# Layer 1's neighbourhood attention on tiles of 8 rows by 16 columns, with the bias table laid out on the host

## The chip, the cores and the metric

One core of a Trainium2 chip runs the whole program in one launch. The time is that of the device in microseconds, from the launch to the end, median of three runs. All inputs start in HBM. Arrays may be laid out anew on the host before the launch; that is not timed, and no arithmetic on input values is done there. Matrix products run in a 32-bit form in which each operand is split into a rounded high part and a rest, so that one product is three: high x high, high x low, low x high.

## The reference

Two blocks of two layers each. The change is in the second layer of the first block: 512 latent tokens on a grid of 8 rows by 64 columns, 256 context tokens, 8 heads of 128 features. With eight rows the row window of 8 is the whole grid, so a query at column c sees all rows, 16 neighbouring columns, and the whole context:

```python
def neighbourhood_attention(q, k, v, k_ctx, v_ctx, rpb):
    ...
    cols = np.arange(GRID_W)                                  # 64
    c_start = np.clip(cols - WIN_C // 2, 0, GRID_W - WIN_C)   # 16 columns from here
    col_mask = (cols[None, :] >= c_start[:, None]) & (cols[None, :] < c_start[:, None] + WIN_C)
    dc_idx = np.clip(cols[None, :] - cols[:, None] + WIN_C - 1, 0, 2 * WIN_C - 2)
    rpb_c = rpb[:, :, dc_idx]
    def row_block(r):
        ...
        s_lat = jnp.einsum('bhqd,bhrkd->bhqrk', q_r, k_b).astype(f32) * scale + bias.astype(f32)
        s_lat = jnp.where(col_mask[:, None, :], s_lat, -jnp.inf).reshape(b, h, GRID_W, wr * GRID_W)
        s_ctx = jnp.einsum('bhqd,bhkd->bhqk', q_r, k_ctx).astype(f32) * scale
        p = jax.nn.softmax(jnp.concatenate([s_lat, s_ctx], axis=-1), axis=-1).astype(v.dtype)
        ...
```

Queries and keys are projections of the normed tokens, normed again per head; the output goes through an output projection.

## The kernel before

Each of the five engines runs a fixed program in the order in which it is written; they wait for each other on semaphores. Weights stream through two slots: SP loads 512 KB into `raw`, ACT rounds it to `w_hi` (L330), POOL computes the rest `w_lo` (L390).

`pe_near`, `act_near` and `dve_near` are the attention of this layer. They walk over 8 heads `e` with five projection items `i` each, and over 32 units `u`, four a head, one for each block of 128 queries. A unit of head e - 1 is worked on behind an item of head e. TensorE does, in this order:

- `item(e, i)`: the projection, 8 x 3 products over the features. i = 0 is the queries (512 columns), 1 and 2 the keys, 3 and 4 the values; the 768 tokens are cut in two thirds of 384 columns (`third_at`, `THIRD`).
- `post(at)`: for queries and keys the sum of the squares over the features (a product with ones, L2424), for values three transposes (L2428).
- `step(u)`, in four of the five rounds: `turn(u - 1)` transposes the probabilities of the last unit (6 blocks, L2437), `scores(u)` makes the scores of the next (L2449, 3 products over 256 context keys and 3 over 512 latent keys), `weigh(u - 1)` multiplies the transposed probabilities with the values (6 products, L2460). `near_order` gives the unit; behind item 3 there is none.

DVE copies items out of PSUM (`evict`, L2576), finishes norms (`finish`: reciprocal L2588 and multiply L2589), makes low parts (`low`, L2594), and for a unit negates and takes the minimum of the scores with the bias table added (`shift`, L2603 and L2604), scales by the inverse sum (`normalise`, L2612), and copies the result out (`take`, L2617). ACT squares (L2511), takes roots (L2520), rounds (L2525), copies the transposes out of PSUM (`copy`, L2531), takes the exponential (L2536), and rounds the next weights in rounds 0, 2 and 4.

The queries of a unit are two grid rows. The bias table `bt` holds for each of the 64 key columns and 120 pairs of head and row distance a value per query; it is made at the start of the stage from the 120 x 31 parameters by 256 small products with a band of ones (`bias` in `pe_near`, L2381), and DVE adds the column mask as it copies it (`bias` in `dve_near`, L2568). These calls stand between the items of head 0. After the last item the units 28 to 31 have no items beside them: `step` is followed by products of the output projection (`out_part`, L2371), and `hold` (L397) puts in products of the identity with itself. Then the output projection goes on at L425.

## Time and profile before

| | us |
|---|---|
| median of three runs | 3625.74 (3624.43 to 3628.43) |
| span of the profiled execution | 3613.9 |
| PE busy | 3486.9 (96%) |
| DVE busy | 1619.4 (45%) |
| ACT busy | 1223.8 (34%) |
| POOL busy | 1173.4 (32%) |

The span is that of one profiled execution, from its first to its last instruction; the profile gives no other time for it, and the launch and the end of the program lie around it. Matmul times overlap, since the next begins while the last one drains: what one costs is read from the start of one to the start of the next. The chain that ended last is 51% issue, 21% PE, 19% POOL and 6% DVE.

### The profile page before, as it was taken

The page shows a single profiled execution, that of the slowest core. Times are in us where ns is not written, and L with a number is a line of the kernel's source. Part 1 is how long each engine was busy: PE and PEld are TensorE (multiplying, and loading weights), DVE is VectorE, ACT ScalarE, POOL GpSimd, SP SyncE. Part 2 cuts the span into 40 slices and gives each one's busy share as a digit, 9 for nine tenths or more (in the row PEclk, how much of TensorE's full clock was granted, in tenths as well). Part 3 has the DMA queues.
Part 4 walks back from the last instruction along what each step waited for, and adds up shares of the span by engine and source line. Part 5 has one row for each costly group of instructions (what it writes and reads, how often), then busy time and mean ns, then how long its engine had stood idle before and what let it go on. Part 6 is the DMA issues. An engine that isn't in the chain of part 4 may idle for free.

```text
span 3613.9 us, 61844 instructions
## 1 busy us (share of the span) xinstructions
PE 3486.9 (96%) x24970; PEld 3053.1 (84%) x24970; DVE 1619.4 (45%) x2762; ACT 1223.8 (34%) x1848; POOL 1173.4 (32%) x812
## 2 busy tenths in 40 slices
PE   8999988889999999999999999999999999999998
PEld 6777878878888888889888888978999999778887
DVE  6966644446220222666662135455512355564121
ACT  4545432233111111455532223255312232542222
POOL 1221122223222233111155454213444432145453
PEclk9999999999999999999999999999999999999999
DMA  5320000001432421111133232112222321123332
GB/s 229 112 70 25 32 2 2 2 25 59 174 110 91 154 86 60 41 42 42 45 96 101 88 104 75 59 48 65 88 93 87 99 70 53 48 76 94 98 93 93
DMA packets 65341, 273.80 MB, mean 76 GB/s; under 512 B 9856, under 2 KB 11008, under 8 KB 62080
## 3 DMA queue, kind: packets, MB, share of 16 engines
q1 hardware_dynamic: 61280, 268.58, 22.4%
q8 instruction: 144, 2.36, 0.3%
q10 hardware_dynamic: 3872, 2.49, 0.2%
q14 instruction: 45, 0.37, 0.0%
HBM read 268.95 MB, written 2.10 MB: 75 GB/s over the span
## 4 chain that ended last, share of the span: by engine, by line
issue 51%; PE 21%; POOL 19%; DVE 6%; ACT 1%; POOLq 0%; PEld 0%; PEldq 0%; DVEq 0%; ACTq 0%
POOL w_lo L390 18%; PE ps L407 10%; PE ps L1488 3%; DVE arena L1776 1%; DVE arena L1762 1%; PE ps L506 1%; PE ps L1998 1%; PE ps L1571 0%; PE ps L2004 0%; DVE arena L1832 0%; PE ps L1549 0%; PE ps L1903 0%; POOLq L385 0%; POOL delta_bufs L2295 0%; DVE arena L1781 0%
## 5 line engine op out<-in xcount | busy, mean ns | idle before, releaser
L390 POOL TENSOR_TENSOR w_lo<-raw,w_hi 128x512 fp32r<-128x512 f32 (+1 forms) x760 | 1101.0, 1469 | 2169.9 <-ACT w_hi L330 2169.9
L330 ACT CAST w_hi<-raw 128x1024 fp32r<-128x1024 f32 (+1 forms) x380 | 419.6, 1104 | 1583.1 <-PE ps L407 1262.7
L407 PE MATMUL ps<-act_hi,w_hi 128*128 128x512 f32 (+2 forms) x2048 | 579.0, 337 | 9.3 <-POOL w_lo L390 3.7
L407 PE MATMUL ps<-act_lo,w_hi 128*128 128x512 f32 (+2 forms) x2048 | 576.8, 336 | 0.0
L407 PE MATMUL ps<-act_hi,w_lo 128*128 128x512 f32 (+2 forms) x2048 | 576.5, 336 | 0.0
L407 PEld LDWEIGHTS ps<-act_hi,w_hi 128*128 128x128 f32 x2048 | 360.1, 188 | 63.3 <-issue 23.5
L407 PEld LDWEIGHTS ps<-act_hi,w_lo 128*128 128x128 f32 x2048 | 362.4, 188 | 41.9
L407 PEld LDWEIGHTS ps<-act_lo,w_hi 128*128 128x128 f32 x2048 | 362.2, 188 | 40.9
L407 PE MATMUL ps<-ff_hi,w_hi 128*128 128x512 f32 (+2 forms) x1056 | 297.1, 336 | 0.0
L407 PE MATMUL ps<-ff_hi,w_lo 128*128 128x512 f32 (+2 forms) x1056 | 297.0, 336 | 0.0
L407 PE MATMUL ps<-ff_lo,w_hi 128*128 128x512 f32 (+2 forms) x1056 | 297.0, 336 | 0.0
L2753 PE MATMUL ps<-act_hi,w_hi 128*128 128x272 f32 (+1 forms) x896 | 265.2, 296 | 0.0
L2753 PE MATMUL ps<-act_lo,w_hi 128*128 128x272 f32 (+1 forms) x896 | 253.8, 283 | 0.0
L2753 PE MATMUL ps<-act_hi,w_lo 128*128 128x272 f32 (+1 forms) x896 | 253.7, 283 | 0.0
L780 DVE TENSOR_TENSOR nscr<-nscr,ps 128x256 f32<-128x256 f32 (+2 forms) x66 | 34.8, 556 | 436.0 <-PE ps L407 436.0
L407 PEld LDWEIGHTS ps<-ff_lo,w_hi 128*128 128x128 f32 x1056 | 186.5, 188 | 21.1
L407 PEld LDWEIGHTS ps<-ff_hi,w_hi 128*128 128x128 f32 x1056 | 186.5, 188 | 20.9
L407 PEld LDWEIGHTS ps<-ff_hi,w_lo 128*128 128x128 f32 x1056 | 186.5, 188 | 20.8
L2753 PEld LDWEIGHTS ps<-act_hi,w_hi 128*128 128x128 f32 x896 | 169.3, 189 | 10.3 <-issue 5.9
L2753 PEld LDWEIGHTS ps<-act_lo,w_hi 128*128 128x128 f32 x896 | 169.4, 189 | 0.9
L2753 PEld LDWEIGHTS ps<-act_hi,w_lo 128*128 128x128 f32 x896 | 169.5, 189 | 0.0
L725 DVE TENSOR_TENSOR nscr<-nscr,ps 128x512 f32<-128x512 f32 (+2 forms) x50 | 26.4, 556 | 315.8 <-PE ps L407 287.5
(495 smaller groups left out, 6249.1 us busy)
## 6 DMA issues: line engine op xcount, KB each, us to landing
raw<-in_gu SPq DMA_DIRECT2D x176, 512.0 KB, 3.5
arena<-in_ada SPq DMA_DIRECT2D x24, 2048.0 KB, 7.8
raw<-in_dn SPq DMA_DIRECT2D x64, 704.0 KB, 4.1
raw<-in_in SPq DMA_DIRECT2D x56, 512.0 KB, 3.5
raw<-in_even_in SPq DMA_DIRECT2D x28, 512.0 KB, 3.5
raw<-in_odd_in SPq DMA_DIRECT2D x24, 512.0 KB, 3.5
raw<-in_out SPq DMA_DIRECT2D x16, 512.0 KB, 3.6
raw<-in_even_out SPq DMA_DIRECT2D x8, 512.0 KB, 3.5
```

The costliest lines, as they stand in the source:

```text
L330: act.copy(w_hi[:, j, 0:cols], raw[:, j, 0:cols]).then_inc(s["hi_ready"], 1)
L390: ins = pool.tensor_tensor(w_lo[:, j, c], raw[:, j, c], w_hi[:, j, c].bitcast(F32), ALU.subtract)
L407: mm = pe.matmul(ps[:, 2 * j + b, 0:cn], wt[:, j, w], acts[:, k, c0:c0 + cn], start=(k == 0 and wt is w_hi and acts is hi), stop=(k == kt ...
L506: mm = pe.matmul(ps[:, 2 * j + b, 0:cn], wt[:, j, w], acts[:, k, c0:c0 + cn], start=(k == 0 and wt is w_hi and acts is hi), stop=(k == KD ...
L725: ins = dve.tensor_tensor(nscr[:, 1, h0:h0 + hn], nscr[:, 0, h0:h0 + hn], ps[:, 2 + b, 0:hn], ALU.mult)
L780: ins = dve.tensor_tensor(nscr[:, 1, h0:h0 + hn], nscr[:, 0, h0:h0 + hn], ps[:, 2 + b, 0:hn], ALU.mult)
L1488: mm = pe.matmul(ps[:, h, 0:cn], wt[:, b % 2, w], a[:, k, c0:c0 + cn], start=(k == 0 and wt is w_hi and a is act_hi), stop=(k == KD - 1 an ...
L1762: ins = dve.scalar_tensor_tensor(acc, gd[:, m, j:j + GN], v("conv", 5 * m + j), acc, ALU.mult, ALU.add)
L1776: dve_link(dve, n, dve.reciprocal(r, r))
L1998: mm = pe.matmul(pblk(2, d, e, b), blk(DEC_B if l % 2 else LAB_B, d, e, b), blk(X, d, e, b), start=True, stop=True)
L2753: mm = pe.matmul(ps[:, h, 0:cn], wt[:, b % 2, w], a[:, k, TOK2 + c0:TOK2 + c0 + cn], start=(k == 0 and wt is w_hi and a is act_hi), stop=( ...
```

## The change

A unit is now a tile of 8 grid rows by 16 grid columns. Its 128 queries have all eight rows, and the key columns in reach are 24 (first and last block) or 32 (the two in the middle), which is 192 or 256 latent keys where there were 512. To make these keys contiguous, tokens are stored by octets of columns: `evict` writes an item of 512 columns in the order octet, row, column in the octet. The values are stored with the last octet first, so that the copy of item 4 is two instructions; `PIECES` says for each block which value tiles and rows its four blocks of probabilities meet. `take` writes the results back in the order of the grid.

The items are cut at the border of context and latent: 512 queries, 512 latent keys, 256 context keys, 256 context values, 512 latent values. The round without a step is that of the context keys (i = 2). Scores of a unit lie in one PSUM bank, its transposes too, and units take turns between two banks. `turn` and `weigh` have 4 products, the exponential and the scaling 448 or 512 columns.

The bias is the same for all blocks up to the mask, because a query sees the same relative columns. The host lays the parameters out as 128 x 2048 values (copies and zeros only); ACT's queue loads them where it loaded the parameters, and DVE adds the masks for three kinds of block in ten instructions (`tables`). The bias products, their semaphores and the band of ones are gone.

```diff
+    cmask = []
+    for block, first, octets in ((1, -1, 4), (0, 0, 3), (3, -1, 3)):
+        q = 16 * block + 8 * (i // 64) + i % 8
+        start = np.clip(q - 8, 0, 48)[:, None]
+        kk = 16 * block + 8 * first + np.arange(8 * octets)[None, :]
+        cmask.append(np.where((kk >= start) & (kk < start + 16), 0.0, -BIG))
...
-        bt = arena[:, 0:120 * 64].rearrange("p (s c) -> p s c", c=64)
+        near_bias = arena[:, 0:2048]
+        near_tables = [(near_bias.rearrange("p (e o t) -> p e o t", e=8, o=4), cmask[0]),
+                       (arena[:, 2048:3584].rearrange("p (e o t) -> p e o t", e=8, o=3), cmask[1]),
+                       (arena[:, 3584:5120].rearrange("p (e o t) -> p e o t", e=8, o=3), cmask[2])]
...
+        NEAR_COLS = (None, (CTX, LAT), (0, CTX), (0, CTX), (CTX, LAT))
...
+            return rows.rearrange("p (o r j) -> p r o j", o=8, r=8)
...
+        KEYS = ((0, 192), (64, 256), (192, 256), (320, 192))
+        PIECES = (((0, 0, None), (P, 1, None), (CTX - 64, 5, 64), (CTX + 64, 2, None)),
+                  ((0, 0, None), (P, 1, None), (CTX, 2, None), (CTX + P, 3, None)),
+                  ((0, 0, None), (P, 1, None), (CTX, 3, None), (CTX + P, 4, None)),
+                  ((0, 0, None), (P, 1, None), (CTX, 4, None), (CTX + P, 5, 0)))
 
         def near_unit(u):
 
-            e, t = u // 4, u % 4
-            j0 = 15 * e + 7 - 2 * t
-            return e, t * P, bt[:, j0:j0 + 8, :].rearrange("p s c -> p (s c)")
+            e, b = u // 4, u % 4
+            k0, kn = KEYS[b]
+            table = near_tables[{0: 1, 3: 2}.get(b, 0)][0]
+            return e, b, CTX + k0, kn, table[:, e].rearrange("p o t -> p (o t)")
 
         def near_order(e, i):
 
-            u = 4 * (e - 1) + (i if i < 3 else i - 1)
-            return None if i == 3 or e == 0 else u
+            u = 4 * (e - 1) + (i if i < 2 else i - 1)
+            return None if i == 2 or e == 0 else u
...
-            def bias(g):
...
             def turn(u, beats=0):
-                if u >= 1:
-                    pe.wait_ge(s["near_copied"], u)
-                hold(pe, beats, 4)
+                if u >= 2:
+                    pe.wait_ge(s["near_copied"], u - 1)
+                hold(pe, beats, 4 + u % 2)
                 pe.wait_ge(s["near_p"], u + 1)
-                for t in range(6):
-                    mm = pe.transpose(ps[:, 4 + t // 4, (t % 4) * P:(t % 4 + 1) * P], near_z[:, u % 2, t * P:(t + 1) * P], ident)
+                for t, (c, _, _) in enumerate(PIECES[u % 4]):
+                    mm = pe.transpose(ps[:, 4 + u % 2, t * P:(t + 1) * P], near_z[:, u % 2, c:c + P], ident)
                 mm.then_inc(s["near_turned"], 1)
...
-                if u >= 1:
-                    pe.wait_ge(s["near_top"], u)
-                else:
-                    pe.wait_ge(s["bt_read"], 16)
-                for b, (k0, kn) in enumerate(BOTH):
+                if u >= 2:
+                    pe.wait_ge(s["near_top"], u - 1)
+                for z0, c0, cn in ((0, 0, CTX), (CTX, k0, kn)):
                     for q, k in ((q_hi, k_hi), (q_lo, k_hi), (q_hi, k_lo)):
-                        mm = pe.matmul(ps[:, 2 + b, 0:kn], q[:, e % 2, q0:q0 + P], k[:, e % 2, k0:k0 + kn],
+                        mm = pe.matmul(ps[:, 2 + u % 2, z0:z0 + cn], q[:, e % 2, b * P:(b + 1) * P], k[:, e % 2, c0:c0 + cn],
...
-                for t in range(6):
-                    mm = pe.matmul(ps[:, 6, 0:P], near_v[:, e % 2, t, :], near_pt[:, u % 2, t * P:(t + 1) * P],
-                                   start=(t == 0), stop=(t == 5))
+                for t, (_, tile, half) in enumerate(PIECES[u % 4]):
+                    rows = slice(0, P) if half is None else slice(half, half + 64)
+                    mm = pe.matmul(ps[:, 6, 0:P], near_v[rows, e % 2, tile, :], near_pt[rows, u % 2, t * P:(t + 1) * P],
+                                   start=(t == 0), stop=(t == 3))
...
-                act.copy(near_pt[:, u % 2, 0:T], ps[:, 4:6, :].rearrange("p a t -> p (a t)")[:, 0:T]).then_inc(s["near_copied"], 1)
+                act.copy(near_pt[:, u % 2, 0:4 * P], ps[:, 4 + u % 2, :]).then_inc(s["near_copied"], 1)
...
+                z = near_z[:, u % 2, 0:CTX + KEYS[u % 4][1]]
...
-            def bias(g):
-                dve.wait_ge(s["bt_ready"], g + 1)
-                c = slice(4 * g, 4 * g + 4)
-                dve.tensor_tensor(bt[:, :, c], ps[:, 2 + g % 4, 0:480].rearrange("p (c s) -> p s c", c=4),
-                                  cmask[:, c].unsqueeze(1).to_broadcast([P, 120, 4]), ALU.add).then_inc(s["bt_read"], 1)
+            def tables(i):
+                whole = near_tables[0][0]
+                if i == 1:
+                    dve.wait_ge(s["rpb_landed"], 16)
+                kind = i % 3
+                table, mask = near_tables[kind]
+                for o in range(table.shape[2]):
+                    cube = lambda a: a.rearrange("p e (r j) -> p e r j", j=8)
+                    ins = dve.tensor_tensor(cube(table[:, :, o]), cube(whole[:, :, o + (1 if kind == 1 else 0)]),
+                                            mask[:, 8 * o:8 * o + 8].unsqueeze(1).unsqueeze(1).to_broadcast([P, 8, 8, 8]), ALU.add)
+                if i == 3:
+                    dve_link(dve, n, ins)
 
             def evict(at):
                 _, cn, dst = near_item(at // ITEMS, at % ITEMS)
                 dve.wait_ge(s["item_done"], at + 1)
                 if at >= ITEMS and at % ITEMS >= 3:
                     dve.wait_ge(s["post_done"], at - ITEMS + 1)
-                dve.tensor_copy(dst, ps[:, item_bank(at), 0:cn]).then_inc(s["item_read"], 1)
+                src = ps[:, item_bank(at), 0:cn]
+                if cn == LAT:
+                    dst, src = by_octets(dst), by_rows(src)
+                if at % ITEMS == 4:
+                    dve.tensor_copy(dst[:, :, 1:8], src[:, :, 0:7])
+                    dst, src = dst[:, :, 0], src[:, :, 7]
+                dve.tensor_copy(dst, src).then_inc(s["item_read"], 1)
...
+                z, bank = near_z[:, u % 2, :], ps[:, 2 + u % 2, :]
+                dve_link(dve, n, dve.tensor_scalar(z[:, 0:CTX], bank[:, 0:CTX], -1.0, None, ALU.mult, ALU.min, accum_out=small[:, 4:5]))
+                dve.tensor_tensor_reduce(z[:, CTX:CTX + kn], bank[:, CTX:CTX + kn], table, -1.0, small[:, 4:5], ALU.add, ALU.min,
                                          small[:, u % 2:u % 2 + 1]).then_inc(s["near_top"], 1)
...
-                dve.tensor_copy(near_mix[:, e, q0:q0 + P], ps[:, 6, 0:P]).then_inc(s["near_taken"], 1)
+                rows = near_mix[:, e].rearrange("p (r b o j) -> p b r o j", r=8, b=4, o=2)[:, b]
+                dve.tensor_copy(rows, ps[:, 6, 0:P].rearrange("p (o r j) -> p r o j", o=2, r=8)).then_inc(s["near_taken"], 1)
 
             for e in range(8):
                 for i in range(ITEMS):
                     at = ITEMS * e + i
                     u = near_order(e, i)
                     evict(at)
-                    if e == 0:
-                        for g in range(4 * i, min(4 * i + 4, 16)):
-                            bias(g)
+                    if e == 0 and 1 <= i <= 3:
+                        tables(i)
...
-                act.dma_start(pa[0:31, 1:121], dram["rpbT"]).then_inc(s["rpb_landed"], 16)
+                act.dma_start(near_bias, dram["rpb"]).then_inc(s["rpb_landed"], 16)
...
+    def near_table(z):
+
+        wide = np.zeros((8, 15, 47), np.float32)
+        wide[:, :, 8:39] = z
+        rows = [wide[:, 7 - r:15 - r, 15 - 8 * o - j:47 - 8 * o - j] for o in range(2) for r in range(8) for j in range(8)]
+        return np.stack(rows).reshape(P, 8, 8, 4, 8).transpose(0, 1, 3, 2, 4).reshape(P, 2048)
```

On ACT, head 1, from the exponential behind item 2 to that behind item 4, before (`arena<-ps,eps_t` is a root, `arena,small<-arena,small` an exponential, ACT_TABLE_LOAD the change of function table between the two):

```order
L2536 ACT_TABLE_LOAD
L2536 ACTIVATE arena,small<-arena,small 128x768 [waits near_top]
L2520 ACT_TABLE_LOAD [waits normed]
L2520 ACTIVATE arena<-ps,eps_t 128x384 [waits post_done]
L2525 CAST near_parts<-arena 128x384 [waits normed]
L2531 COPY arena<-ps 128x768 [waits near_out,near_turned]
L2525 CAST near_parts<-arena 128x384 [waits normed]
L330 CAST w_hi<-raw 128x1024 [waits w_landed1,item_done]
L2536 ACT_TABLE_LOAD
L2536 ACTIVATE arena,small<-arena,small 128x768 [waits near_top]
```

And now, from the root of the context keys behind item 3 to the exponential behind item 4:

```order
L2505 ACTIVATE arena<-ps,eps_t 128x256 [waits normed,post_done]
L2516 COPY arena<-ps 128x512 [waits near_turned]
L2510 CAST near_parts<-arena 128x512 [waits normed]
L2521 ACT_TABLE_LOAD
L2521 ACTIVATE arena,small<-arena,small 128x512 [waits near_top]
L2516 COPY arena<-ps 128x512 [waits near_out,near_turned]
L2510 CAST near_parts<-arena 128x256 [waits normed]
L326 CAST w_hi<-raw 128x1024 [waits w_landed1,item_done]
L2521 ACTIVATE arena,small<-arena,small 128x448 [waits near_top]
```

The last root now stands in a round that has a step, ahead of its exponential, and the exponential of the round of item 4 follows without a change of table.

On TensorE, the work between the third and the fourth item of head 0 before (L2424 the sum of squares, L2381 the bias products):

```order
L2381 MATMUL ps<-pa,base 64x120 [waits scaled_ready]
L2381 MATMUL ps<-pa,base 64x120 x15
L2424 MATMUL ps<-arena,base 128x512 [waits square_ready]
L2381 MATMUL ps<-pa,base 64x120 [waits bt_read]
L2381 MATMUL ps<-pa,base 64x120 x7
```

And now this place and the next two follow-ups, with the items between them left out:

```order
L2417 MATMUL ps<-arena,base 128x512 [waits square_ready]
...
L2417 MATMUL ps<-arena,base 128x512 [waits square_ready,post_read]
L2417 MATMUL ps<-arena,base 128x256 [waits square_ready,post_read]
...
L2422 MATMUL ps<-base,arena 128x128 [waits item_read,post_read]
L2422 MATMUL ps<-base,arena 128x128
```

Nothing stands any more between an item's sum of squares and the next item.

## Rows read from the trace of the kernel before

**Rows 1.** Busy time by stretches: stretch, length, engines (instructions), clock, DMA share, GB/s

```profile
core 0: us, PE busy (x) PEld busy (x) DVE busy (x) ACT busy (x) POOL busy (x), PEclk, DMA share, GB/s
1512.00:1767.00 255.00, 253.94 (x1533) 229.53 (x1532) 167.87 (x298) 152.50 (x204) 52.92 (x42) 1.00 0.15 44
1767.00:1799.00 32.00, 27.92 (x192) 23.45 (x191) 17.74 (x48) 16.80 (x27) 2.50 (x2) 1.00 0.08 20
1484.00:1487.70 3.70, 3.70 (x64) 3.54 (x61) 2.60 (x5) 0.74 (x2) 0.00 (x0) 1.00 0.42 140
1487.80:1491.20 3.40, 3.40 (x12) 3.40 (x12) 3.37 (x2) 0.00 (x0) 0.00 (x0) 0.52 0.00 0
```

**Rows 2.** PE's timeline, one round: start, duration, engine, line, operation, count, idle before

```profile
1560.14 0.42 PE L2390 MATMUL ps<-act_hi,w_hi 128*128 128x384 f32 x1
...
1564.40 0.81 PE L2424 MATMUL ps<-arena,base 128*128 128x384 f32 x2
1565.12 0.85 PE L2437 MATMUL ps<-base,arena 128*128 128x128 f32 x6
1565.72 1.30 PE L2449 MATMUL ps<-near_parts 128*128 128x256 f32 x6
1566.90 1.58 PE L2460 MATMUL ps<-arena 128*128 128x128 f32 x12
1568.23 0.42 PE L2390 MATMUL ps<-act_hi,w_hi 128*128 128x384 f32 x1
```

**Rows 3.** ACT's timeline, the copy of the same round

```profile
1566.00 0.80 ACT L2531 COPY arena<-ps 128x768 f32<-128x768 f32 x1 [0.17 <-PE ps L2437]
```

**Rows 4.** PE's timeline, the scores of unit 0 and of unit 27

```profile
1511.81 1.29 PE L2449 MATMUL ps<-near_parts 128*128 128x256 f32 x6
...
1767.05 1.30 PE L2449 MATMUL ps<-near_parts 128*128 128x256 f32 x6
```

**Rows 5.** PE's timeline in the feed-forward ahead, pairs of 256 and 512 columns

```profile
1450.12 0.51 PE L407 MATMUL ps<-ff_hi,w_lo 128*128 128x256 f32 x2
1450.46 0.51 PE L407 MATMUL ps<-ff_hi,w_hi 128*128 128x256 f32 x2
```

**Rows 6.** ACT's groups by form, 1445 to 1800: count, busy us, mean ns, idle before

```profile
L2520 ACT ACT_TABLE_LOAD x21 | 26.9, 1283 | 0.4
...
L2520 ACT ACTIVATE arena<-ps,eps_t 128x384 f32<-128x384 f32 x16 | 9.3, 583 | 35.2 <-PE ps L2424 35.2
...
L2520 ACT ACTIVATE arena<-ps,eps_t 128x512 f32<-128x512 f32 x8 | 5.5, 687 | 22.4 <-PE ps L2424 22.4
```

**Rows 7.** DVE's groups by form, 1445 to 1800

```profile
L2588 DVE RECIPROCAL arena<-arena 128x512 f32<-128x512 f32 x8 | 26.8, 3347 | 0.0
...
L2568 DVE TENSOR_TENSOR arena<-ps,base 128x480 f32<-128x480 f32 x16 | 10.4, 657 | 6.6 <-PE ps L2381 6.6
...
L2594 DVE TENSOR_TENSOR near_parts<-arena,near_parts 128x384 fp32r<-128x384 f32 x16 | 8.8, 552 | 0.0
...
L2594 DVE TENSOR_TENSOR near_parts<-arena,near_parts 128x512 fp32r<-128x512 f32 x8 | 5.5, 685 | 0.0
```

**Rows 8.** DVE's groups by form, whole span

```profile
L560 DVE TENSOR_TENSOR nscr<-nscr 128x512 f32<-128x512 f32 x16 | 26.2, 1637 | 0.0
```

**Rows 9.** PE's timeline, bias products at the start of the stage

```profile
1483.53 3.50 PE L2381 MATMUL ps<-pa,base 31*64 31x120 f32 x64
1486.96 0.44 PE L2390 MATMUL ps<-act_hi,w_hi 128*128 128x384 f32 x1
```

**Rows 10.** DVE's timeline, its first copy of the stage

```profile
1479.95 0.69 DVE L2576 COPY arena<-ps 128x512 f32<-128x512 f32 x1
```

**Rows 11.** POOL's timeline

```profile
1480.34 2.50 POOL L390 TENSOR_TENSOR w_lo<-raw,w_hi 128x512 fp32r<-128x512 f32 x2 [22.03 <-ACT w_hi L330]
```

**Rows 12.** PE's timeline, turns of units 27 and 31, and the output projection

```profile
1772.73 0.87 PE L2437 MATMUL ps<-base,arena 128*128 128x128 f32 x6 [0.94 <-DVE arena L2612]
...
1793.60 0.85 PE L2437 MATMUL ps<-base,arena 128*128 128x128 f32 x6 [0.47 <-DVE arena L2612]
...
1798.81 0.47 PE L425 MATMUL ps<-act_hi,w_hi 128*128 128x512 f32 x1 [0.26 <-DVE act_lo L916]
```

85 lines of the change are left out of this document (25 added, 60 removed).

## The prediction

> **What bounds the kernel now.** I read the page's first part: PE is busy nearly the whole span, the others half of it or less, so a change pays where it takes PE time or shortens a wait of PE. The busy time by stretches then shows that the attention of layer 1, from 1512 to 1767 us, has PE at 253.9 of 255 us, DVE at 168 and ACT at 153, and the clock at 1.00 [rows 1]. PE sets the pace; DVE and ACT have a third free on the mean, which says nothing yet of the short stretches. Third, PE's own timeline of one round, for the start-to-start times (busy times of overlapping matmuls are longer than what they cost) [rows 2].
>
> I call a round one projection item with what follows it: the item, its follow-up (`post`), and a step: `turn` of the last unit (6 transposes), `scores` of the next, `weigh` of the last. In the round shown [rows 2] the item takes 1560.14 to 1564.40, the follow-up to 1565.12, `turn` 0.60 us, `scores` 1.18, `weigh` 1.33: a step is 3.11 us. From the first scores to those of unit 27 it is 1511.81 to 1767.05 [rows 4]: 255.2 us, 27 steps, 37.8 a head of four.
>
> **The steady part, per step.** Price of one instruction, start to start:
> - `weigh`: 6 products in 1.33 us, 0.222 each. Two fewer: -0.44.
> - `turn`: 6 transposes in 0.60 with the entry to them, so at most 0.10 each; I take 0.095: two fewer, -0.19.
> - `scores`: an item of 384 columns is 24 products in 4.26 us with some 0.1 of entry (1560.14 to 1564.40) [rows 2], 0.1735 each, so at most 0.45 ns a column. At the full clock of 2.4 GHz, which these rows show [rows 1], one column is 0.42 ns; I take that. Three products shrink from 512 to 256 columns (-0.32) or to 192 (-0.40), half the units each: -0.36.
>
> PE's own work would fall by 0.99 a step. But `weigh` waits for ACT's copy of the transposes, and the trace has the two nearly equal: `turn` starts at 1565.12, the copy runs 1566.00 to 1566.80 [rows 3], `weigh` starts at 1566.90 [rows 2]. After the change the transposes end 0.19 earlier; the copy of 512 columns instead of 768 costs 0.80 - 256 x 0.81 ns = 0.59, the slope from 687 against 583 ns for 512 and 384 columns [rows 6]; then 0.10 to `weigh`. That is 0.85 - 0.19 + 0.04 + 0.59 + 0.10, about 1.37 us after `turn` began, where PE alone would be through at 1.2. The copy becomes the late one: turn to weigh 1.76 to 1.37, saved 0.39, and with `weigh` 0.83 to 0.84 a step. In the round after the latent keys' item ACT has a root of 512 columns (0.69) ahead of the copy, and I take 0.69 there. Of 27 steps 7 are of that kind: 20 x 0.84 + 7 x 0.69 = **21.6 us**. Bounds: 27 x 0.99 = 26.9 if the copy delays nothing; 14 if DVE is late by 1 us in each of 7 heads besides.
>
> The items: a head had one of 512 columns and four of 384, and has three of 512 and two of 256. In the feed-forward ahead a 256 and a 512 together take 0.347 us (1450.12 to 1450.46) [rows 5], which is twice the 0.1735 of 384 columns: nothing gained or lost, items of about 5.55 and 2.98 us. Root sums and transposes after them keep their columns.
>
> What becomes late in the short rounds? I lay out one head from the end of the latent keys' item (t = 0). PE: root sums, step (`weigh` ends 3.3), context keys' item to 6.3, sums to 7.2, context values' item to 10.1, sums, step to 12.9, latent values' item to 18.4. DVE: copy out, shift of the scores to 3.2, reciprocal of 512 columns (3.35) [rows 7] and multiply to 7.2, normalise 7.8, copies to 8.4, second reciprocal and multiply to 12.4, low parts and copy to 13.3, shift to 14.2, third reciprocal (256 columns) to 16.4, normalise to 17.0. The transposes that need it stand at 18.65 in PE's queue: 1.6 us to spare. The nearest miss is the square of the context keys, ready on ACT at about 9.8 with PE asking at 10.1. So DVE is behind for ten us, and nothing waits. ACT is helped: in the order of after a head has 2 loads of the exp table and 2 of the root's where it had 3 and 3, 1.28 us each [rows 6].
>
> **The start of the stage.** 256 products for the bias table go. 64 take 3.4 us (1483.53 to 1486.96, the next item) [rows 9], 0.054 each, 13.8 in all; but the first 32 stand where PE waits for the normed activations. DVE's chain comes next, from 1479.95 [rows 10]: two copies (1.2), three table adds (0.6 each: 1.8), reciprocal and multiply (4.05), copy and three adds (2.1), second reciprocal and multiply (4.05), low parts, copy, four adds (3.3), third (2.2), the rest 2.0: near_lo stands at about 1500.7. PE: the root sums wait for squares that ACT makes only after rounding the first normed item, so PE idles 3 us near 1487 to 1490, then has two items of 5.55 and two follow-ups: scores at 1502.0. The table adds read both operands in SBUF while POOL writes low parts from 1480.34 for 2.5 us [rows 11]. A DVE add of 512 columns with two SBUF operands takes 685 ns here [rows 7] and 1637 in the feed-forwards, where POOL is at work beside it [rows 8]; I add 1.0 for it. The Trainium skill (SBUF — State Buffer, "Who interferes with whom") says that a DVE instruction with two SBUF inputs contends with a GpSimd one that reads SBUF; these rows agree. The clock: in the trace it is 0.52 from 1487.8 to 1491.2, behind 64 small bias products [rows 1], at a cost of some 1.7. With those gone and idle time in their place I expect such a stretch again, half of it behind a wait: +0.8. Scores at 1503.8 instead of 1511.81: **-8.0 us** (bounds -5.5 and -10.5).
>
> The table's load, 1 MB on ACT's queue where 15 KB went, is issued some 27 us before its first reader: the same ring moved 140 GB/s beside other work [rows 1], 7.5 us. Hidden. `base` is 57 KB shorter at the kernel's start: 0 to -0.3; I take 0.
>
> **The end of the stage.** From unit 28 on there is no projection to fill PE, and the period is a loop: turn, scores, shift, exp, normalise, turn. From turn 27 at 1772.73 to turn 31 at 1793.60 [rows 12] four periods of 5.2. Each loses 0.19 (turn), 0.32 to 0.40 (scores), 0.27 to 0.33 (DVE on fewer columns, 1.04 ns each from 685 and 552 ns for 512 and 384 [rows 7]), 0.21 to 0.26 (exp, at ACT's slope) and 0.15 (normalise): 1.15 to 1.35. The `hold` products of step 29 cut one of them; I take -5.0 for four, -0.84 behind the last (turn, copy, weigh), and -1.7 ahead of turn 27, where ACT's table load of 1.28 goes. **-7.5 us** (6 to 8.5).
>
> **Sum.** -21.6 - 8.0 - 7.5 = -37.1. The profiled span is 3613.9; launch and end lie around it, as the median of the runs, 3625.74, is 11.8 above; the same 11.8 is kept. 3625.7 - 37.1 = 3588.6.
>
> **Rivals.**
> 1. The copy delays nothing (ACT's copy is shorter than its slope says): 26.9 for 21.6. 3583.3.
> 2. Permuted access costs DVE. Copies out and `take` now write and read in runs of 8 floats. The trace has a worse pattern: the bias add read PSUM at a stride of 120 floats and wrote runs of 4, at 657 ns for 480 columns [rows 7], no slower a column than a plain add. At half pace 2560 columns a head would add 2.7 us to DVE, the square would miss by 0.4 a head, start and tail lose 2: 3593.5. By the Trainium skill (SBUF — State Buffer, "Door 1: The DMA port swizzle") each access that crosses into another 16-byte line pays; the row of the bias add doesn't show it, and the measurement decides.
> 3. The table adds meet POOL each time: 10 x (1.64 - 0.69) = 9.5 at the start, the -8.0 gone: 3598.
> 4. The clock falls once a head, for PE now waits for the copy: 7 x 1.7 = 12: 3600.5. Against it: the waits are 0.1 to 0.3 us, and PE has longer ones from 1767 to 1799, at clock 1.00 [rows 1].
> 5. Slower: the permuted writes on DVE cost what its slowest operation does, 6.5 ns a column (3347/512) [rows 7]. 2560 columns add 14 us to DVE's 25 a head (168 us over 6.75 heads [rows 1]), 39 against the 37.8 of a head now: DVE bounds the stage, +8 there, +10 at the start and end: 3644. It decides from about 5.5 ns a column on; the bias add at 1.4 speaks against it.
>
> **Chances.** Forecast 60% (its own range 3584 to 3594), rival 1 14%, 2 8%, 3 6%, 4 8%, 5 4%. Range 3580 to 3599. Runs of this kernel lie within some 0.1%, so 0.2% (7 us) is what can be told from no change: faster 0.95, same 0.01, slower 0.04.
>
> **What would show it.** Start of the first scores product near 1504, 27 steps later near 1737.5, first product of the out-projection behind the last unit, 1798.81 now [rows 12], near 1762. Steps of 2.2 to 2.3 us with `weigh` 1.35 to 1.4 after `turn`; if it is 1.2, rival 1. Permuted copies of 512 columns near 0.7 us on DVE, else 2 or 5. Table adds near 0.7, else 3. The granted clock in 40 slices shows 4. I am wrong if PE waits for DVE in the short rounds by more than 1 us a head.

## The result, and the profile after

The changed kernel takes 3591.39 us (median of four runs, 3589.48 to 3598.37) against 3625.09 of the kernel before beside it: ratio 0.9915, 95% interval 0.9901 to 0.9929, 33.7 us less. The forecast was 3588.6, 2.8 below the median.

The profiled spans, 3613.9 and 3590.6, differ by 23.3 only, so they can't be subtracted. The first copy of the stage starts at 1479.95 before [rows 10] and 1487.15 after, 7.2 us later, though nothing ahead of it was changed but a shorter constant; behind the stage another 3.4 us go the same way. The clock is 0.99 for 1.00 from 10 to 1440 us by the view of stretches: the profiled execution of before had less time at the lower level there. All that follows is measured inside the stage, from four marks that both kernels have: DVE's first copy, PE's first product of `scores(0)` and of `scores(27)`, and the first product of the output projection. In the trace of after, the first row is from DVE's timeline, the other three from PE's:

```profile
1487.15 1.29 DVE L2574 COPY arena<-ps 128x512 f32<-128x512 f32 x2
```

```profile
1510.72 0.91 PE L2441 MATMUL ps<-near_parts 128*128 128x256 f32 x6
...
1746.82 0.92 PE L2441 MATMUL ps<-near_parts 128*128 128x256 f32 x6
...
1772.10 0.47 PE L421 MATMUL ps<-act_hi,w_hi 128*128 128x512 f32 x1
```

Against rows 4, 10 and 12 they give this table:

| part | before | after | difference | predicted |
|---|---|---|---|---|
| start: first copy to scores(0) | 31.86 | 23.57 | -8.29 | -8.0 |
| steady: scores(0) to scores(27) | 255.24 | 236.10 | -19.14 | -21.6 |
| tail: scores(27) to the output projection | 31.76 | 25.28 | -6.48 | -7.5 |
| whole | 318.86 | 284.95 | -33.91 | -37.1 |

The sum of the parts, -33.9, agrees with the medians, -33.7. By stretches (to be set beside [rows 1]) PE is still the one that is always busy, DVE rose from 168 to 183 and ACT fell from 153 to 133:

```profile
core 0: us, PE busy (x) PEld busy (x) DVE busy (x) ACT busy (x) POOL busy (x), PEclk, DMA share, GB/s
1462.00:1512.00 50.00, 43.88 (x219) 35.92 (x220) 43.17 (x62) 20.06 (x33) 10.97 (x9) 0.93 0.16 53
1512.00:1767.00 255.00, 251.99 (x1499) 214.25 (x1499) 182.85 (x347) 132.66 (x214) 53.79 (x42) 1.00 0.14 46
```

PE's timeline of two rounds (to be set beside [rows 2]; products of the projection items are left out), the round after the latent keys' item and a plain one:

```profile
1552.42 1.02 PE L2417 MATMUL ps<-arena,base 128*128 128x512 f32 x2
1553.28 0.60 PE L2431 MATMUL ps<-base,arena 128*128 128x128 f32 x4
1553.63 0.95 PE L2441 MATMUL ps<-near_parts 128*128 128x256 f32 x6
1554.74 1.52 PE L2453 MATMUL ps<-arena 128*128 128x128 f32 x8 [0.16 <-issue]
1556.01 0.36 PE L2385 MATMUL ps<-act_hi,w_hi 128*128 128x256 f32 x1
...
1563.14 0.60 PE L2431 MATMUL ps<-base,arena 128*128 128x128 f32 x4
1563.49 0.96 PE L2441 MATMUL ps<-near_parts 128*128 128x256 f32 x6
1564.46 1.13 PE L2453 MATMUL ps<-arena 128*128 128x128 f32 x8
1565.35 0.48 PE L2385 MATMUL ps<-act_hi,w_hi 128*128 128x512 f32 x1
```

`weigh` is counted from its start to that of the next item. The plain round is as forecast: `turn` to `weigh` 1.32 (1.37 expected), `weigh` 0.89, a step of 2.21. The other has `weigh` at 1.27, and so has every unit with b = 0 and b = 3; before, all took 1.33 with six products. That was in no term of the sum. A head from scores to scores takes 35.07 after and 37.77 before.

DVE's and ACT's groups by form, 1445 to 1800 (to be set beside [rows 6] and [rows 7]):

```profile
L2593 DVE TENSOR_TENSOR near_parts<-arena,near_parts 128x256 fp32r<-128x256 f32 x8 | 12.1, 1506 | 0.0
...
L2574 DVE COPY arena<-ps 128x512 f32<-128x512 f32 x16 | 11.0, 690 | 34.9 <-PE ps L2385 34.9
...
L2617 DVE COPY arena<-ps 128x128 f32<-128x128 f32 x32 | 9.0, 281 | 2.1 <-PE ps L2453 2.1
...
L2558 DVE TENSOR_TENSOR arena<-arena,base 128x512 f32<-128x512 f32 x10 | 7.6, 821 | 0.0
...
L2572 DVE COPY arena<-ps 128x448 f32<-128x448 f32 x8 | 5.0, 624 | 2.9 <-PE ps L2385 2.9
...
L2574 DVE COPY arena<-ps 128x64 f32<-128x64 f32 x8 | 1.7, 214 | 0.0
```

```profile
L2516 ACT COPY arena<-ps 128x512 f32<-128x512 f32 x32 | 18.7, 584 | 64.2 <-PE ps L2431 64.2
```

The permuted copies of queries and latent keys (L2574, 512 columns) take 690 ns, the price of the plain one in [rows 10]. The latent values go in two pieces, 448 columns in 624 ns and 64 in 214. `take` (L2617) takes 281 ns. None is near half pace, so rivals 2 and 5 are out. ACT's copy takes 584 ns, where the slope gave 0.59.

A low part of 256 columns (L2593) takes 1506 ns, twice what one of 512 takes. All eight begin while an instruction of POOL is running, and end 0.28 us behind its end. The first of them, the row of POOL beside it, and the same low part in e6_tables_late, where it began 0.12 us before POOL's and took 0.41 (DVE, POOL, DVE, POOL):

```profile
1509.03 1.52 DVE L2593 TENSOR_TENSOR near_parts<-arena,near_parts 128x256 fp32r<-128x256 f32 x1
...
1508.98 5.25 POOL L386 TENSOR_TENSOR w_lo<-raw,w_hi 128x512 fp32r<-128x512 f32 x4 [8.18 <-ACT w_hi L326]
...
1505.92 0.41 DVE L2593 TENSOR_TENSOR near_parts<-arena,near_parts 128x256 fp32r<-128x256 f32 x1
...
1506.04 1.44 POOL L386 TENSOR_TENSOR w_lo<-raw,w_hi 128x512 fp32r<-128x512 f32 x1 [6.79 <-ACT w_hi L326]
```

The start, PE's and then DVE's timeline:

```profile
1488.55 1.12 PE L2417 MATMUL ps<-arena,base 128*128 128x512 f32 x2 [0.77 <-ACT arena L2496]
1490.53 0.39 PE L2385 MATMUL ps<-act_hi,w_hi 128*128 128x256 f32 x1 [0.86 <-POOL w_lo L386]
...
1498.66 0.67 PE L2417 MATMUL ps<-arena,base 128*128 128x256 f32 x2 [2.63 <-ACT arena L2496]
```

```profile
1488.35 3.28 DVE L2558 TENSOR_TENSOR arena<-arena,base 128x512 f32<-128x512 f32 x3
...
1495.93 1.88 DVE L2558 TENSOR_TENSOR arena<-arena,base 128x512 f32<-128x512 f32 x3
...
1502.72 2.48 DVE L2558 TENSOR_TENSOR arena<-arena,base 128x512 f32<-128x512 f32 x4
```

```profile
1491.30:1494.60 3.30, 3.30 (x17) 3.30 (x17) 3.30 (x2) 0.00 (x0) 0.00 (x0) 0.51 0.50 159
```

PE now has gaps where the bias products stood: 0.77, 0.86 and 2.63 us. The first three table adds meet POOL's `w_lo` and take 3.28 for 1.88; POOL's two instructions, from 1487.54, take 2.94 for 2.50 [rows 11], and the gap of 0.86 is PE waiting for them. The clock is at its lower level, 1.2 GHz (0.51), from 1491.3 to 1494.6, right behind the first two gaps: what the last row, of the view by stretches, shows. DVE's last low part ends at 1510.55 and `scores(0)` starts at 1510.72, so DVE's chain and PE's end almost together.

### The profile page after: what moved, and what is told of

The parts are those of the page before. It is cut to its first block, busy times and chain, and to the rows that moved or that the text cites. A ratio compares the mean times of both kernels' runs of the same rounds, so it can differ in the third digit from the quotient of the medians.

```text
span 3590.6 us, 60934 instructions
## 1 busy us (share of the span) xinstructions
PE 3459.0 (96%) x24522; PEld 3012.8 (84%) x24522; DVE 1618.9 (45%) x2764; ACT 1189.9 (33%) x1834; POOL 1174.1 (33%) x812
## 4 chain that ended last, share of the span: by engine, by line
issue 51%; PE 22%; POOL 19%; DVE 6%; ACT 1%; POOLq 0%; PEld 0%; PEldq 0%; DVEq 0%; ACTq 0%
POOL w_lo L386 18%; PE ps L403 10%; PE ps L1484 3%; DVE arena L1772 1%; DVE arena L1758 1%; PE ps L502 1%; PE ps L1994 1%; PE ps L1567 1%; PE ps L2000 0%; DVE arena L1828 0%; PE ps L1545 0%; POOL delta_bufs L2291 0%; POOLq L381 0%; PE ps L1555 0%; DVE arena L1777 0%
## 5 line engine op out<-in xcount | busy, mean ns | idle before, releaser
L403 PEld LDWEIGHTS ps<-ff_lo,w_hi 128*128 128x128 f32 x1056 | 186.5, 188 | 20.9
L403 PEld LDWEIGHTS ps<-ff_hi,w_lo 128*128 128x128 f32 x1056 | 186.5, 188 | 20.9
L403 PEld LDWEIGHTS ps<-ff_hi,w_hi 128*128 128x128 f32 x1056 | 186.5, 188 | 20.9
L2752 PEld LDWEIGHTS ps<-act_hi,w_hi 128*128 128x128 f32 x896 | 171.0, 191 | 10.2 <-issue 5.9
```

Of the source, the lines that this page charges most:

```text
L403: mm = pe.matmul(ps[:, 2 * j + b, 0:cn], wt[:, j, w], acts[:, k, c0:c0 + cn], start=(k == 0 and wt is w_hi and acts is hi), stop=(k == kt ...
L2752: mm = pe.matmul(ps[:, h, 0:cn], wt[:, b % 2, w], a[:, k, TOK2 + c0:TOK2 + c0 + cn], start=(k == 0 and wt is w_hi and a is act_hi), stop=( ...
```

## The experiments

Differences of a few us are near the scatter of whole runs, so most runs were read by the marks; e10_all_half, e2_half_copy, e3_more_scores, e5_narrow_alone, e4_bias_back, e6_tables_late and e8_start were executed once, the others four times. Steady is scores(0) to scores(27), a head is from scores(8) to scores(12) and the like in the middle, where all heads of a kernel agree within 0.07.

| kernel | start | steady | tail | a head | `turn` to `weigh`, b = 0 / others | `weigh`, b = 0, 1, 2, 3 |
|---|---|---|---|---|---|---|
| before | 31.86 | 255.24 | 31.76 | 37.77 | 1.76 / 1.76 | 1.33 in all |
| after | 23.57 | 236.10 | 25.28 | 35.07 | 1.47 / 1.32 | 1.27, 0.89, 0.89, 1.25 |
| after_again | 24.67 | 235.63 | 25.29 | 35.05 | | |
| e1_full_rows | 24.32 | 230.69 | 24.92 | 34.28 | 1.47 / 1.32 | 0.89 in all |
| e10_all_half | 23.45 | 236.47 | 25.08 | 35.1 | 1.47 / 1.32 | 1.06 in all |
| e2_half_copy | 24.20 | 230.22 | 24.86 | 34.21 | 1.26 / 1.11 to 1.15 | 1.27, 0.84, 0.89, 1.25 |
| e3_more_scores | 24.60 | 238.13 | 26.70 | 35.38 | 1.50 / 1.46 to 1.51 | 1.23, 0.81, 0.83, 1.19 |
| e7_gaps | 24.21 | 230.71 | 25.13 | 34.29 | 1.47 / 1.32 | 0.89 in all |
| e7_again | 24.24 | 230.73 | 25.13 | 34.27 to 34.31 | 1.47 / 1.32 | 0.89 in all |
| e5_narrow_alone | 31.82 | 232.80 | 25.29 | 34.33 | 1.47 / 1.32 to 1.36 | 0.89 in all |
| e4_bias_back | 31.41 | 235.63 | 25.27 | 35.05 | | |
| e6_tables_late | 24.24 | 235.63 | 25.27 | 35.05 | | |
| e8_start | 24.08 | 235.75 | 25.29 | 35.07 | | |
| e9_all | 23.12 | 230.76 | 25.12 | 34.3 | | |

**The 64-row products: all rows.**

```diff
-                    rows = slice(0, P) if half is None else slice(half, half + 64)
+                    rows = slice(0, P)
```

> The changed kernel with every product of weigh on all 128 rows; the changed kernel has one product of 64 rows in the units b = 0 and b = 3 of each head. The output is wrong there, since 64 rows of a tile's transposes are weighed that don't belong. Theory A (a product of 64 rows among ones of 128 costs some 0.4 us): weigh takes 0.89 us start to next item in all units, where the changed kernel has 1.25 to 1.35 for b = 0 and b = 3; from scores(0) to scores(27) 236.1 becomes 231 (13 such units x 0.36 to 0.45). Theory B (the longer weigh there comes from what stands around it, such as the rows' place in PSUM or the copy): weigh keeps 1.25 to 1.35 for b = 0 and 3, and the stretch stays within 0.5 of 236.1.

`weigh` is 0.89 in every unit and the steady part 230.69: 5.4 less than after, 4.9 less than after_again. 7 x 0.38 + 6 x 0.36 is 4.8, so the second is the price, and most of the other 0.5 is the first head, 33.90 in after and 33.55 in after_again. Theory A. Whole: 3587.59, ratio 0.9904 (0.9887 to 0.9920).

**All products on 64 rows.**

```diff
-                    rows = slice(0, P) if half is None else slice(half, half + 64)
+                    rows = slice(0, 64)
```

> The changed kernel with every product of weigh on rows 0 to 63 alone, four of them a unit; half of the sums is left out of the output. Theory A1 (each product of 64 rows costs the 0.4 us more): weigh takes 0.89 + 4 x 0.4 = 2.5 us, the stretch from scores(0) to scores(27) grows from 236.1 to some 231 + 27 x 1.6 = 274. Theory A2 (the change between 64 and 128 rows costs it, once or twice a unit): weigh takes 1.25 to 1.35 in all units, with the two changes at its start and end, the stretch 231 + 27 x 0.4 = 242. Theory B (rows don't matter): 0.89 or less in b = 1 and 2, as now, and 236.

`weigh` is 1.06 in all units: not 2.5 (A1 is out) and not 0.89 (B is out). A2, the change of the row count as the cost, is nearest, but it had 0.36 to 0.46 on top of 0.89 where 0.17 came (the stretch of 236.5 is theory B's number, but made up of 26 `weigh` that are each 0.17 longer than full ones). The weight loads show where it lies. PEld's timeline in the changed kernel, a unit b = 0 with the 64-row product third, and the same in the kernel with 64 rows throughout, a plain round:

```profile
1554.71 0.52 PEld L2453 LDWEIGHTS ps<-arena 128*128 128x128 f32 x4 [0.34 <-issue]
...
1555.35 0.29 PEld L2453 LDWEIGHTS ps<-arena 64*128 64x128 f32 x2
...
1555.77 0.30 PEld L2453 LDWEIGHTS ps<-arena 128*128 128x128 f32 x2
1555.98 0.19 PEld L2385 LDWEIGHTS ps<-act_hi,w_hi 128*128 128x128 f32 x1
```

```profile
1563.77 0.31 PEld L2441 LDWEIGHTS ps<-near_parts 128*128 128x128 f32 x2
1564.27 0.96 PEld L2453 LDWEIGHTS ps<-arena 64*128 64x128 f32 x8 [0.18 <-issue]
1565.35 0.19 PEld L2385 LDWEIGHTS ps<-act_hi,w_hi 128*128 128x128 f32 x1
```

Each product is two loads, 0.11 us apart (four from 1554.71, the last begins at 1555.04). The 64-row load then begins 0.31 behind its forerunner, and the 128-row load behind it (1555.46 to 1555.77) 0.31 as well: each change of the row count costs 0.20 beyond the usual spacing. A half tile on rows 64 to 127 (b = 0) and one on rows 0 to 63 (b = 3) cost nearly the same, 0.38 and 0.36, so the place of the rows isn't it. Why a change costs this is not shown: a PE matmul of this form is recorded at 275 ns, so a load that waits for the running product to end would look like this, but no row names the reason. With 64 rows throughout, the change into `weigh` falls in the wait for ACT's copy and only the one out of it shows: 1.06 for 0.89. In the changed kernel both show.

The Trainium skill (TensorE: Matmul & The Clock Gate, "The mechanism") says that a weight load overlaps running products only when its row group doesn't conflict or it goes to the spare weight buffer, and elsewhere in that page ("Step-by-step: what each phase is for") that a load's timing goes by its columns and the row count doesn't matter. For one row count throughout this case agrees with the second (loads 0.11 apart at 64 and at 128 rows); at a change of the count the next load begins 0.20 us later.

**ACT's copy halved.**

`weigh` reads the two copied blocks twice, so it still has four products:

```diff
-                    mm = pe.matmul(ps[:, 6, 0:P], near_v[rows, e % 2, tile, :], near_pt[rows, u % 2, t * P:(t + 1) * P],
+                    mm = pe.matmul(ps[:, 6, 0:P], near_v[rows, e % 2, tile, :], near_pt[rows, u % 2, t % 2 * P:(t % 2 + 1) * P],
...
-                act.copy(near_pt[:, u % 2, 0:4 * P], ps[:, 4 + u % 2, :]).then_inc(s["near_copied"], 1)
+                act.copy(near_pt[:, u % 2, 0:2 * P], ps[:, 4 + u % 2, 0:2 * P]).then_inc(s["near_copied"], 1)
```

> The changed kernel where ACT copies only 256 of the 512 transposed columns (0.38 us for 0.59) and weigh reads these twice; the output is wrong by that. Theory A (ACT's copy ends last, the step as predicted): turn to weigh falls from 1.32 to 1.2 or so in the plain rounds, where PE's own order becomes the late one, and from 1.48 to 1.28 in the rounds with the 512 root before the copy; from scores(0) to scores(27) 236.1 becomes 236.1 - 20 x 0.12 - 7 x 0.2 = 232.3. Theory B (PE's own instructions set it already, the copy is hidden): turn to weigh stays 1.32, the stretch within 0.7 of 236.1.

ACT's and PE's timelines:

```profile
1562.97 0.37 ACT L2516 COPY arena<-ps 128x256 f32<-128x256 f32 x1
```

```profile
1562.33 0.60 PE L2431 MATMUL ps<-base,arena 128*128 128x128 f32 x4
...
1563.48 1.09 PE L2453 MATMUL ps<-arena 128*128 128x128 f32 x8
```

The copy is 0.22 shorter and `weigh` starts 0.17 to 0.21 sooner. The steady part falls by 5.9, more than the 3.8 expected: 27 x 0.2 is 5.4, and `weigh` of b = 1 is 0.05 shorter. The copy is the late one in every round (theory A), and PE's own order would have had `weigh` at 1.11, not at 1.2.

**Three more score products a unit.**

```diff
-                for z0, c0, cn in ((0, 0, CTX), (CTX, k0, kn)):
+                for z0, c0, cn in ((0, 0, CTX), (0, 0, CTX), (CTX, k0, kn)):
```

> The changed kernel that makes the context scores twice: 3 more products of 256 columns a unit, 0.12 us each start to start, 0.36 a unit. Theory A (weigh waits for ACT's copy, with 0.2 us of PE's time free before it, as the half copy showed): turn to weigh grows by 0.16 in the plain rounds and 0.0 to 0.1 in those after the latent keys; from scores(0) to scores(27) 236.1 + 20 x 0.16 + 7 x 0.0 = 239.3. Theory B (PE's own work sets the step): 236.1 + 27 x 0.36 = 245.8.

238.13, 2.0 above after and 2.5 above the other runs of the same stage: theory A. Of 0.36 us of work a unit 0.08 is paid. `turn` to `weigh` rises to 1.47 in the plain rounds, which is 1.11 + 0.36, and `weigh` falls to 0.82 for 0.89 when nothing is waited for before it. PE had idle time there that it could fill almost free.

**Fewer columns alone, on the kernel before** (the edit, shortened):

```diff
-                for t in range(6):
+                for t in range(4):
...
-                for b, (k0, kn) in enumerate(BOTH):
+                for b, (k0, kn) in enumerate(((0, CTX), (CTX, KN[u % 4]))):
...
-                act.copy(near_pt[:, u % 2, 0:T], ps[:, 4:6, :].rearrange("p a t -> p (a t)")[:, 0:T]).then_inc(s["near_copied"], 1)
+                act.copy(near_pt[:, u % 2, 0:4 * P], ps[:, 4, :]).then_inc(s["near_copied"], 1)
```

> The kernel before with one part of the change alone: 4 transposes and 4 products of weigh a unit, scores against 192 or 256 of the 384 latent keys, ACT's copy 512 columns wide, exp and normalise on 448 or 512. Items of 384 columns, the table products on PE and the order stay as before; no mask is added, keys are left out, so the output is wrong. Theory A (the gain of the steady part and the tail comes from the fewer columns; the start's from the table products): from the first copy of the stage to scores(0) 31.9 us as before; from scores(0) to scores(27) 255.2 falls by what the changed kernel shows without its 64-row products, 24.5, to 230.7; scores(27) to the out-projection 31.8 to 25. Theory B (the items of 512 and 256 columns for those of 384 and the order have a part in it): the stretch comes out 1.5 us or more from 230.7.

Start 31.82, tail 25.29, a head 34.33, as theory A has it (34.28 in e1_full_rows). The steady part is 2.1 above 230.7, which is theory B's mark; but the middle heads hardly differ. 1.7 of it lies in the first head (34.90 against 33.17 in e1_full_rows), the rest is 0.05 to 0.1 a head. So items of 512 and 256 columns for 384 are worth next to nothing in the steady state, as assumed. What the first head has in the old order is a wait of PE for POOL's `w_lo`, in the item behind `scores(0)`: 1.44 us here (1518.52) and 1.06 before, where after has 0.12 and e1_full_rows none. PE's timeline of before:

```profile
1514.16 0.45 PE L2390 MATMUL ps<-act_hi,w_hi 128*128 128x384 f32 x1 [1.06 <-POOL w_lo L390]
```

The end of this wait was in no term of the forecast; no run shows which part of the new order ends it.

**The bias products put back.** The 16 groups are called at their old places again (the calls are left out here), into free banks, and nobody reads them:

```diff
+            def bias(g):
+                for q in range(4):
+                    c = 4 * g + q
+                    for h in range(2):
+                        pe.matmul(ps[64 * h:64 * h + 64, 2 + g % 4, 120 * q:120 * q + 120], base[0:31, 63 - c:127 - c],
+                                  vec[0:31, 1 - h:121 - h], start=True, stop=True)
```

> The changed kernel with the table products put back at their old places on PE, in banks that other work leaves free, and read by nobody. The output stays. Theory A (PE's own work sets the start of the stage, as predicted): from the first copy to scores(0) 23.6 us becomes 23.6 + 13.8 - some 3 that lie in PE's wait for the squares, plus a stretch of half clock of up to 1.7: 32 to 36. Theory B (DVE's chain of reciprocals and table adds sets it, and PE's products were hidden beside it): 23.6 to 26.

Start 31.41, just under theory A's 32: 7.8 us more for products that take 13.8. Theory B (23.6 to 26) is out. PE's timeline:

```profile
1488.93 1.86 PE L2384 MATMUL ps<-vec,base 31*64 31x120 f32 x32
1490.71 1.13 PE L2426 MATMUL ps<-arena,base 128*128 128x512 f32 x2
1491.77 3.50 PE L2384 MATMUL ps<-vec,base 31*64 31x120 f32 x64
...
1500.62 3.50 PE L2384 MATMUL ps<-vec,base 31*64 31x120 f32 x64
1504.04 0.70 PE L2426 MATMUL ps<-arena,base 128*128 128x256 f32 x2
```

They lie partly where after has its gaps of 0.77, 0.86 and 2.63 us, and the start is within 0.5 of before's, less than the 1.2 by which the starts of after's kind differ among themselves. The start's gain is these products, as far as can be told.

**Seven of the ten table adds later.**

```diff
-                    if e == 0 and 1 <= i <= 3:
-                        tables(i)
+                    if e == 0 and i == 1:
+                        tables(1)
...
+                    if at == ITEMS:
+                        tables(2)
+                        tables(3)
```

> The changed kernel with 7 of its 10 table adds moved from the first head's items to behind the copy of the second head's first item; DVE has 3 at the old place. The whole computation. Theory A (PE sets the start: its waits for the squares, then two long items): the last low part is ready some 5 us earlier, but scores(0) stands behind the same items on PE, so from the first copy to scores(0) 23.6 becomes 23.0 to 23.6; and scores(0) to scores(27) stays 236.1 or grows by up to 1 where the unit waits for the adds. Theory B (DVE's chain sets it): 7 x 0.65 to 0.8 us come off the start, 18 to 19.5.

Start 24.24, no gain: theory A, though above its 23.6. DVE's last low part is done at 1506.3, and the first scores stand at 1510.77 behind PE's item. The steady part is none the longer.

The adds are not free of effect, though. In e10_all_half, whose start differs from after's in nothing but has no stretch at the lower clock (1.00 from 1487.1 to 1510.6), PE is sooner and waits for DVE's last low part:

```profile
1510.56 0.61 PE L2441 MATMUL ps<-near_parts 128*128 128x256 f32 x3 [0.56 <-DVE near_parts L2593]
```

So DVE's chain holds the start of this order at 23.4 us, where PE's own, at the full clock, would allow some 22.6 (its last follow-up starts at 1509.40 and takes 0.35 elsewhere: an estimate).

**Another order on PE in the first head,** with the late adds:

```diff
                     elif i == 2:
                         post(0)
-                    elif i == 3:
                         post(1)
+                    elif i == 4:
                         post(2)
-                    elif i == 4:
                         post(3)
```

> The changed kernel with the late table adds of before and another order on PE in the first head: both key root sums stand ahead of the context values' item, and the latent root sums and the values' transposes behind the two values' items. The whole computation. Theory A (PE's waits for squares set the start: 3.2 us idle before the third root sum, and item 3 behind it in the queue): these waits fall under the items; the last low part on DVE, some 19.3 us after the first copy by its own chain, becomes the late one: scores(0) 19 to 20.5 instead of 24.2. Theory B (the wait moves along, since the squares and roots are behind the root sums that now stand between the items): 23 or more. From scores(0) to scores(27) 235.6 to 237 by both.

24.08: no gain, and both theories miss. B's wait didn't move along, the 3.2 us before the third root sum are gone; the time went to a third place. PE's timeline, and then two stretches, the columns those of the view by stretches:

```profile
1486.77 2.08 PE L2417 MATMUL ps<-arena,base 128*128 128x512 f32 x2 [0.77 <-ACT arena L2495]
1490.24 2.05 PE L2417 MATMUL ps<-arena,base 128*128 128x512 f32 x2 [1.39 <-ACT arena L2495]
```

```profile
1485.90:1496.10 10.20, 8.05 (x24) 5.37 (x24) 10.16 (x9) 4.40 (x7) 3.33 (x3) 0.50 0.14 51
1496.00:1500.00 4.00, 4.00 (x22) 3.43 (x22) 3.56 (x4) 0.00 (x0) 2.12 (x2) 0.98 0.19 29
```

The clock stays at the lower level for 10.2 us, where after has some 3.4: each root sum takes 2.05 for 1.12 or less, and the 256-column item runs at half pace. By an estimate from these rows that is 0.9 and 0.5 for the root sums and some 2.3 for the item, nearly the 4 us that were to be won. Whether the new order is the cause isn't shown. The clock had fallen by 1485.9, where the order is still the old one, behind waits of 0.3 us for the normed activations; what differs is that it came back later. With the gaps below (e9_all) it was low for 10.1 us too, from 1487.8, 1.6 us ahead of the first copy, and the start came to 23.12. The old order has stretches of 3.4 or 6.8 us: 3.4 in all in after (start 23.57) and e7_again (24.24), about 9 in all in after_again (24.67).

**No half tiles, the whole result (gaps).** The 192 keys of b = 0 and 3 are laid out with a gap of 64 filled by DVE, and `PIECES` takes all rows of tile 5 there (the edit, shortened):

```diff
+        LEAD, GAPS = (64, 0, 0, 0), (CTX, None, None, CTX + 192)
...
-                for z0, c0, cn in ((0, 0, CTX), (CTX, k0, kn)):
+                for z0, c0, cn in ((0, 0, CTX), (CTX + LEAD[b], k0, kn)):
...
+                if GAPS[u % 4]:
+                    dve.memset(z[:, GAPS[u % 4]:GAPS[u % 4] + 64], BIG)
```

> The whole computation, without half tiles: for b = 0 and b = 3 the scores of the 192 latent keys are placed so that the missing 64 are a gap that DVE fills with the value that the exponential turns into nothing; exp and normalise are always 512 columns wide, and the four products of weigh have 128 rows. It adds one DVE fill of 64 columns (0.1 us or less), 64 columns to exp and normalise in every second unit (0.06 each), and no PE work. Theory A: as e1, from scores(0) to scores(27) 231, and the tail from there to the out-projection 25.3 - 2 x 0.4 + 2 x 0.2 = 24.9; the whole 5 us shorter than the changed kernel's 3591.4, so some 3586. Theory B (half rows don't matter): 236 to 237 and 3591 or more.

230.71, tail 25.13, 3586.88 us, ratio 0.9900 (0.9882 to 0.9917): theory A. The next three were run beside one another, four executions each:

> The changed kernel once more, beside the next three on one chip, since their differences are near what separates one execution from the next. Median near 3591.4; from the first copy to scores(0) 23.5 to 24.6, to scores(27) 235.6 to 236.1, to the out-projection 25.3, by how many stretches of half clock fall into the start.

> The gap version again, beside the changed kernel on one chip: if the 64-row products cost 5.4 us and nothing else differs, the median lies 5 to 6 us below that of the changed kernel (by theory B, that the earlier difference of 4.5 us was chance, within 1).

> The gap version (no half tiles), the late table adds and the new order of the first head together; the whole computation. Theory A: start 19 to 20.5, scores(0) to scores(27) 230.7 to 231.7, tail 25.1: the stage ends 9 us sooner than in the changed kernel, and the median lies 8 to 10 us below that of the changed kernel beside it, some 3582. Theory B (what the start gains is lost in the first head, whose units wait for the table adds): steady part 234 or more, the median 5 us below.

| kernel | median us (range) | ratio to before, 95% interval |
|---|---|---|
| after_again | 3593.32 (3587.08 to 3597.99) | 0.9908, 0.9892 to 0.9925 |
| e7_again | 3585.48 (3582.08 to 3587.36) | 0.9890, 0.9873 to 0.9906 |
| e9_all | 3584.02 (3581.72 to 3587.47) | 0.9888, 0.9872 to 0.9905 |

The gap version lies 7.8 us below the changed kernel here and 4.5 below its first run (1.7, when each is set against the kernel before that ran beside it), around the 5 of the marks. The intervals of the ratios overlap; it is the marks that settle it, 4.9 to 5.5 us in two profiles of each. It does the whole computation and is the better kernel. The combined one is 1.5 us below that: its start is 1.1 shorter and its steady part equal, so neither theory's number came; within the scatter the two can't be told apart.

## Why the prediction was right, and where it was off

- **What bounds the stage, the copy as the late one.** Right, and the step was nearly exact: 1.32 for 1.37 (its terms add up to 1.39). Rival 1 (1.2, the copy delays nothing) is out by e2_half_copy: it delays by 0.2. (27 x 0.99 in its sum is 26.7, not 26.9.)
- **Steady, -21.6; -19.1 came.** The term of `weigh` was mis-sized: "6 products in 1.33 us, 0.222 each. Two fewer: -0.44" holds for 128-row products and was applied to units with a 64-row one. Those lose only 0.06 to 0.08. e1_full_rows measures it: 4.9 to 5.4 us of the stretch, 0.77 to 0.79 a head. Without it the steady part would be -24.6, 3 us more than forecast: 0.05 a step at `turn` to `weigh` (1.3), 1.2 behind `scores(0)`, nearly all of it the wait for POOL's `w_lo` that is gone, and 0.7 in follow-ups and items, less 0.4 because the stretch holds 26 `weigh` where 27 were counted. Errors of opposite sign; the forecast's closeness owes something to luck.
- **The items cost nothing.** Right within 0.1 a head (e5_narrow_alone, the middle heads).
- **Nothing is late in the short rounds.** Right: PE waits for DVE in no middle round; e6_tables_late, e4_bias_back and e8_start give the middle heads the same 35.04 to 35.07.
- **Start, -8.0; -8.29 came.** Eight profiles of kernels that share this start give 23.45 to 24.67, so the range of the gain is 7.2 to 8.4; the shortest is the one without a stretch at the lower clock, the two longest have most of it, about 9 us. The parts on PE were placed nearly right: the wait for the third square, 2.63 us, ends 11.5 us behind the first copy, where 7 to 10 was forecast (1487 to 1490 against 1479.95), and the square stands behind ACT's rounding, as said. The adds beside POOL cost 1.4 for 1.0. The stretch at the lower clock came, some 3.4 us long, and set PE's chain back by 0.9 where 0.8 was priced (the item behind the third square starts 11.8 us behind the first copy, and 10.9 in e10_all_half, which has no such stretch). DVE's chain was mis-sized: the last low part was to stand 20.8 us behind the first copy, or 21.8 with the 1.0 for the adds, and stands at 23.4: 0.4 more for the adds and 1.1 for the low part itself beside POOL. PE's chain was priced too long by a little (23.9 for 23.6 with the stretch; some 22.6 without it), so e10_all_half has PE waiting for DVE, and its start is only 0.1 shorter than after's. Rival 3 (the adds meet POOL each time) is out: three of ten did.
- **The table's load is hidden.** Right: 4.7 us from issue to landing by the DMA view, and DVE's adds follow its copies without a wait. (The 140 GB/s of [rows 1] are the whole core's, not one ring's.)
- **Tail, -7.5; -6.5 came.** Turn 27 follows scores(27) by 3.85 for 5.68: -1.8 (-1.7 expected). The four periods take 16.9 for 20.9: -4.0, where -5.0 stood. The last three lose 1.2 to 1.4 each, as priced (4.07, 4.03 and 3.85 from turn to turn); it is the first that fell short, 4.95 for 5.16. PE's timeline of after has 0.72 us of it in one wait, for a low part of 256 columns beside POOL, and the half tiles have some 0.2 (the four take 16.74 in e1_full_rows). In e5_narrow_alone, where the last low part has 384 columns and meets nothing, the four take 15.9, the -5.0 of the forecast. From turn 31 to the projection it is 4.53 for 5.21, -0.7 (-0.84 expected).

PE's rows, turns 27 and 31 and the wait:

```profile
1750.67 0.60 PE L2431 MATMUL ps<-base,arena 128*128 128x128 f32 x4
1751.99 0.93 PE L2441 MATMUL ps<-near_parts 128*128 128x256 f32 x6 [0.72 <-DVE near_parts L2593]
...
1767.57 0.63 PE L2431 MATMUL ps<-base,arena 128*128 128x128 f32 x4
```

- **Rival 4, the clock once a head.** Out: the granted clock is 1.00 from 1512 to 1767.
- **"The same 11.8 is kept".** Wrong as a reading, harmless in the sum. Only 2.06 us lie around a span (3592.66 for the span of 3590.6). So the profiled execution of before took about 3615.9 by that (an estimate) and was quicker than its median. The excess stood on both sides of the sum, so it fell out.

## What to carry to other kernels

Price a product by its own shape and by its neighbours': in a chain of 128-row products one of 64 rows cost 0.36 to 0.38 us more than a full one, and filling the tile with columns that weigh nothing was cheaper than skipping them. When work is taken off the engine that bounds, look at what it covered (here 6 of 13.8 us) and at what the clock does around the gaps that it leaves: a start with one wait less came out 0 to 1 us shorter, with the clock at its lower level for 10 us. When the profiles of two kernels are compared, set marks on both sides of the change, since the unchanged parts of these differed by 10 us.
